# Loading expert weights of a mixture-of-experts kernel in 16 KB rows, one expert's matrix per transfer, and giving ring places back whole

## The reference

```python
def hierarchical_moe(h, w_group, b_group, w_router, b_router, w_gate, w_up, w_down):
    ...
    e_id = g_idx[:, None] * EXPERTS_PER_GROUP + top_i.astype(jnp.int32)
    ...
    def expert_block(args):
        xb, e = args
        return (jax.nn.silu(xb @ w_gate[e]) * (xb @ w_up[e])) @ w_down[e]
    ys = lax.map(expert_block, (xs, block_e)).reshape(P, D)
    out = jnp.zeros((N, D), ys.dtype).at[slot_tok].add(ys * slot_w[:, None].astype(ys.dtype))
```

## Time and profile before

| | |
|---|---|
| median of 3 runs | 1418.24 us (1414.12 to 1418.97) |
| span of the profiled execution, first to last instruction | 1412.1 us |
| expert loop of layer 0, of layer 1 | 207.4 to 689.0 us, 915.7 to 1397.0 us |
| TensorE busy | 1298.4 us, 92% |
| weight load busy | 638.1 us, 45% |
| VectorE, ScalarE, GpSimd busy | 34%, 16%, 3% |
| moved by DMA | 489.84 MB, mean 347 GB/s |
| expert weights | 3 x 64 transfers of 2048 KB for each matrix kind, 402.7 MB in 192 transfers |

### The profile page before, as it was taken

The page is one execution under the profiler, slowest core; times in us unless marked ns, Lnnn a source line. Parts: engine busy times, 40 slices in busy tenths (PEclk is TensorE's granted clock), DMA queues, the critical chain, the costliest instruction groups (busy, mean ns, idle before and its releaser), DMA issues.

```text
span 1412.1 us, 17373 instructions
## 1 busy us (share of the span) xinstructions
PE 1298.4 (92%) x6934; PEld 638.1 (45%) x6934; DVE 480.3 (34%) x1239; ACT 227.7 (16%) x523; POOL 35.6 (3%) x75
## 2 busy tenths in 40 slices
PE   5998979999899999899889999889998999998998
PEld 3875543334344334334368555433334333334433
DVE  1188253333323333333311143542323232323232
ACT  1013341000100000100223244310001000001000
POOL 1001120000000000000000000200000000000000
PEclk8999999999999999999999999899999999999999
DMA  9968358999999999999973373579999999999980
GB/s 343 382 229 334 158 233 334 417 415 421 418 413 418 415 420 420 418 413 374 408 278 119 119 312 165 235 294 413 417 419 420 418 414 417 420 418 416 417 353 31
DMA packets 82589, 489.84 MB, mean 347 GB/s; under 512 B 11489, under 2 KB 11634, under 8 KB 33394
## 3 DMA queue, kind: packets, MB, share of 16 engines
q1 hardware_dynamic: 76480, 486.62, 84.4%
q10 hardware_dynamic: 6066, 2.64, 0.7%
HBM read 488.20 MB, written 1.05 MB: 346 GB/s over the span
## 4 chain that ended last, share of the span: by engine, by line
PE 77%; ACT 7%; DVE 7%; issue 3%; ACTq 2%; SPq 1%; DMA 1%; POOL 0%; DVEq 0%
PE psum L1256 77%; ACT phase_region L703 3%; DVE phase_region L905 3%; ACTq L539 2%; DVE x_tokens L1069 2%; ACT phase_region L712 1%; DMA weight_ring<-in_w_ada 1%; SPq L422 1%; ACT phase_region L715 1%; PE psum L1318 0%; ACT ada_partials L582 0%; ACT h_or_mix_T L574 0%; ACT phase_region L563 0%; DVE phase_region L840 0%; ACT phase_region L717 0%
## 5 line engine op out<-in xcount | busy, mean ns | idle before, releaser
L1256 PE MATMUL psum<-weight_ring,phase_region 128*64 128x512 f32 (+1 forms) x3264 | 700.8, 600 | 64.6 <-ACT phase_region L715 41.6
L1256 PEld LDWEIGHTS psum<-weight_ring,phase_region 128*64 128x64 f32 (+1 forms) x3264 | 243.3, 136 | 490.7 <-issue 440.5
L1256 PE MATMUL psum<-phase_region 128*128 128x128 bf16 (+4 forms) x2064 | 255.3, 284 | 5.2 <-POOL phase_region L492 0.9
L1256 PEld LDWEIGHTS psum<-phase_region 128*128 128x128 bf16 (+2 forms) x2064 | 153.2, 117 | 135.3 <-issue 85.3
L1122 DVE TENSOR_TENSOR phase_region<-psum,gate_rows 128x512 f32<-128x512 f32 x64 | 44.3, 692 | 238.6 <-PE psum L1256 238.6
L1256 PE MATMUL psum<-h_or_mix_T,weight_ring 128*128 128x256 f32 (+1 forms) x520 | 117.3, 385 | 5.5 <-DVE h_or_mix_T L849 3.4
L703 ACT ACTIVATE phase_region<-psum,shift,scale 128x128 f32<-128x128 f32 x136 | 51.2, 457 | 439.0 <-PE psum L1256 439.0
L1256 PEld LDWEIGHTS psum<-h_or_mix_T,weight_ring 128*128 128x128 f32 x520 | 100.6, 198 | 19.6 <-DVE h_or_mix_T L849 3.5
L1115 DVE SCALAR_TENSOR_TENSOR phase_region<-phase_region,psum 128x512 f32<-128x512 f32 x32 | 33.7, 1054 | 205.2 <-PE psum L1256 205.2
L1256 PE MATMUL psum<-weight_ring,h_or_mix_T 128*128 128x512 f32 x224 | 102.7, 610 | 0.0
L1069 DVE TENSOR_TENSOR x_tokens<-psum,x_tokens 128x512 f32<-128x512 f32 x136 | 93.6, 690 | 24.6 <-PE psum L1256 24.6
(11 more groups left out here) (172 smaller groups left out, 559.6 us busy)
## 6 DMA issues: line engine op xcount, KB each, us to landing
weight_ring<-in_moe_w_gate SPq DMA_DIRECT2D x64, 2048.0 KB, 9.4
weight_ring<-in_moe_w_up SPq DMA_DIRECT2D x64, 2048.0 KB, 12.5
weight_ring<-in_moe_w_down SPq DMA_DIRECT2D x64, 2048.0 KB, 11.5
weight_ring<-in_w_ada SPq DMA_DIRECT2D x12, 3072.0 KB, 13.0
weight_ring<-in_w_ada SPq DMA_DIRECT2D x12, 1024.0 KB, 15.8
weight_ring<-in_odd_w_in SPq DMA_DIRECT2D x6, 2048.0 KB, 12.6
weight_ring<-in_even_w_in SPq DMA_DIRECT2D x4, 2048.0 KB, 23.6
weight_ring<-in_even_w_out SPq DMA_DIRECT2D x2, 2048.0 KB, 9.9
```

Of the source, the lines that this page charges most:

```text
L1256: return pe.matmul(out_, lhsT, rhs, start=first, stop=last, **kw)
```

## The change

A transfer now brings the whole matrix of one expert, 16 KB a partition in one row; the slab of a pair is still two transfers of 2 MB on the same two semaphores. SyncE issues both when the whole slab has been used; the semaphores `half_used` are gone. TensorE waits for both transfers before the first product of a slab, and `narrow` runs all k for output half 0, then all k for output half 1.

```diff
-                words = slice(half * KD * F // 2, (half + 1) * KD * F // 2)
-                sp.dma_start(pair_slab(n)[:, :, words], src[L, :, bass.ds(pair * 2, 2), words]).then_inc(
+                sp.dma_start(pair_slab(n)[:, half:half + 1, :], src[L, :, bass.ds(pair * 2 + half, 1), :]).then_inc(
                     (slab_in, rest_in)[half][n % RING], 16)
...
                     pairs = turn * UNROLL + (EP * L + k // 3 + 1)
-                    sp.wait_ge(half_used[k % 3], pairs)
-                    load_pair_half(L, k + RING, 0, turn * UNROLL + (k + RING) // 3)
                     if k % 3 < 2:
                         sp.wait_ge((gate_done, up_done)[k % 3], pairs)
                     else:
                         sp.wait_ge(down_done, pairs * 2)
-                    load_pair_half(L, k + RING, 1, turn * UNROLL + (k + RING) // 3)
+                    for half in range(2):
+                        load_pair_half(L, k + RING, half, turn * UNROLL + (k + RING) // 3)
...
-                def widen(bank, w, xt, done, half=None, second=None):
+                def widen(bank, w, xt, done):
 
                     for k in range(KD):
-                        if second is not None and k == KD // 2:
-                            pe.wait_ge(*second)
                         for e in range(2):
                             ins = mm(PS[e * SLOT:(e + 1) * SLOT, bank, :], xt[:, k, e * SLOT:(e + 1) * SLOT],
                                      w[:, e, k * F:(k + 1) * F], k == 0, k == KD - 1, skip_group_check=True)
-                        if half is not None and k == KD // 2 - 1:
-                            ins.then_inc(half, 1)
                     ins.then_inc(done, 1)
...
                         pe.wait_ge(slab_in[slabs[0] % RING], land[0])
-                        widen(0, pair_slab(slabs[0]), XT[:, j % 2], gate_done, half_used[0],
-                              (rest_in[slabs[0] % RING], land[0]))
+                        pe.wait_ge(rest_in[slabs[0] % RING], land[0])
+                        widen(0, pair_slab(slabs[0]), XT[:, j % 2], gate_done)
...
                         pe.wait_ge(slab_in[slabs[2] % RING], land[2])
-                        for h in range(2):
-                            ins = narrow(pair_slab(slabs[2]), range(KF // 2), h, None)
-                        ins.then_inc(half_used[2], 1)
                         pe.wait_ge(rest_in[slabs[2] % RING], land[2])
                         for h in range(2):
-                            narrow(pair_slab(slabs[2]), range(KF // 2, KF), h, down_done)
+                            narrow(pair_slab(slabs[2]), range(KF), h, down_done)
```

More of the change, by code:

```diff
@@ L263, in build_trunk @@
         xt_act = sem("xt_act")
-        half_used = [sem(f"{w}_half_used") for w in ("gate", "up", "down")]
         gate_done = sem("gate_done")
@@ L1599, in moe @@
                         pe.wait_ge(slab_in[slabs[1] % RING], land[1])
-                        widen(1, pair_slab(slabs[1]), XT[:, j % 2], up_done, half_used[1],
-                              (rest_in[slabs[1] % RING], land[1]))
+                        pe.wait_ge(rest_in[slabs[1] % RING], land[1])
+                        widen(1, pair_slab(slabs[1]), XT[:, j % 2], up_done)
                         pe.wait_ge(slots_built, i * (2 * UNROLL) + 2 * ((EP + 1) * L + j + 2))
```

## The result

The changed kernel takes 1431.31 us in the median (1430.27 to 1432.62), the kernel before 1418.28 us; the ratio is 1.0104, with an interval of 1.0082 to 1.0126. It is slower by 13 us, where I had forecast no change, 1418 us in a range of 1410 to 1427.

A forecast was written before the change was run, and what follows sets the result against it. TensorE's own chain, 30.14 us a pair, was taken as the bound, with DMA only keeping up. The 1412.1 us span plus 0 for each of five points, with the median 6.1 us above, gave 1418 us, range 1410 to 1427.

The forecast's parts named there:

- point 2: TensorE waiting for both transfers before a slab: cost 0; bounds a gain of 0, a loss of 11 us.
- Point 1: SyncE's later issue of a slab's first transfer: 0 on the path, at least 13.8 us in hand at every slab.
- Point 3: SyncE's longer wait: only the same slab's two transfers queue behind it, cost 0.
- Point 4: Order of `narrow`: VectorE's first evacuation can start 3.7 us after down starts instead of 5.4; gain 0.
- Point 5: 16 KB rows: 426 GB/s, 7.7 ns fixed cost a packet, 11.8 us of DMA time saved, 0 on the path.
- The sign by which I meant to see it: DMA share in a mid-loop pair down from 1.00 to about 0.98 while GB/s stays.
- A: Rival: 16 KB rows run slower, below 405 GB/s TensorE waits in the loops; 1440 or 1467 us; chance 0.11.
- B: Rival: DMA truly bounds the loops, so its 11.8 us saving comes back, 1406 us; chance 0.06.
- C: Rival: ring reserve smaller than worked out, DMA pauses over 14 us stop TensorE; 1425 us or more; chance 0.02.
- D: Rival: scatter alone carries the median over 7 us in either direction; chance 0.01 each way.
- weight-load rule: Skill's rule judging TensorE by its weight loads' busy share, here 45%, so not full; the prediction didn't follow it.

The follow-up runs named there:

- experiment 6: Changed kernel with only the wait for the down slab's second transfer moved ahead of the slot-weight waits: 1418.31 us, ratio 1.0012.
- experiment 2: Changed kernel with 8 KB rows of both experts per transfer again, all else as changed: 1430.59 us, ratio 1.009.
- experiments 9 and 10: ScalarE copies the turned operands before spreading tokens: on the changed kernel 1386.57 us, ratio 0.9794; on the kernel before 1385.18 us, ratio 0.9792.
- Experiments 4 and 7: Changed kernel with SyncE's first load held back: 1432.26 us; kernel before with one idle extra wait at the head of down: 1429.91 us.
- 3: Kernel before with TensorE waiting for the down slab's second transfer at its head: 1427.30 us, ratio 1.0068.
- experiment 1: Changed kernel with both waits for the down slab moved ahead of the slot-weight waits: 1421.77 us, ratio 1.0022.
- experiment 8: Kernel before with its one wait for the down slab's first transfer moved ahead of the slot-weight waits: 1417.63 us, ratio 1.0007.
- experiment 11: Kernel before with three more waits, on semaphores reached at program start, at the head of every down slab: 1415.79 us, ratio 0.9999.

## Why the prediction was wrong

**The step that failed is point 2.** "Does a fulfilled wait itself cost?" I answered it from a row in which the three waits of down and gate lie inside a run of products, and there they cost nothing (13.95 us). The new wait lies at the head of down, behind a wait that TensorE really waits for, and there it adds 0.10 us to the gap (1.97 against 1.87 us). The quoted order showed this: the register instruction with the operands' waits, and the product with two waits behind it. I read it for what was waited for, and not for what has to be done after the release. I had the two gaps in front of me too: the earlier trace rows has 1.7 and 1.9 us, a difference between pairs that I did not ask about. Its cost as such is small, 8 x 0.1 us. The rest comes by the clock: 5 falls x 1.70 us = 8.5 us, together 9.3 us, against 9.2 us by which the loops grew in the windows (4.0 + 5.2). My bound for this point, 0.12 us for a slab and 11 us in all, comes near the loss only by luck: it stood for a cost of the waits themselves in 96 slabs, and the runs show 0.8 us for that.

**The clock was read as a constant.** I noted 1.00 in the earlier trace rows as a fact of the loop; it was a state that held by about 0.1 us of gap (none of 1.87 us brought a fall, 34 of 48 of 1.97 us did). No rival had the clock in it.

**Point 1 held.** Two issues take 0.87 us, as the queue of the changed kernel shows; landing took at most 16.0 us, where I had 16.4:

```profile
417.66 0.87 SPq L386 DMA_DIRECT2D weight_ring<-in_moe_w_down  x2
...
DMA to landing us min/median/max: 7.5/11.7/16.0
```

**Point 3 held**: experiment 6 keeps it and costs nothing. **Point 4 held**: the first evacuation starts 3.69 us after down, the combine when down ends:

```profile
1414.29 7.09 PE L1253 MATMUL psum<-weight_ring,phase_region 128*64 128x512 f32 x32 [1.73 <-ACT phase_region L712]
...
1421.31 3.96 PE L1253 MATMUL psum<-phase_region 128*128 128x512 f32 x8
...
1417.98 0.69 DVE L1119 TENSOR_TENSOR phase_region<-psum,gate_rows 128x512 f32<-128x512 f32 x1 [4.67 <-PE psum L1253]
```

**Point 5 held**: 429 GB/s measured, 426 forecast, and zero on the path. The fixed cost of a packet worked out from the saturated rates is 2 x 8192 x 16 / 422 - 16384 x 16 / 429 = 10.1 ns. It hangs on one GB/s: other stretches of the same loops show 427 and 428 GB/s in 16 KB rows, against 422 in 8 KB rows, which gives 7 to 9 ns. So my 7.7 ns can stand. The Trainium skill ("DMA: Bandwidth & Descriptors", Why small descriptors are slow) has about 3 cycles a packet, 3.5 ns by the estimate of the prediction; the measurement is larger and decides. The sign by which I meant to see it failed: the DMA share of a mid-loop pair stayed at 1.00.

**Rivals.** A, slower rows, fell with 429 GB/s and experiment 2. B, DMA as the true bound, fell with experiments 9 and 10: a shorter gap alone made both faster by 2.1%. C, a smaller reserve, fell: no slab was waited for. D, scatter, fell: all runs of the changed kernel, in two series, lie between 1428.89 and 1432.62 us. My answer to the weight-load rule in B, to go by the timeline's holes, was right as to the bound. The slower result had none of the reasons I had priced.

**What stays open.** In the first two traces the loops explain 9.2 of 13.0 us. The head, 4.2 us longer there, is chance: in the repeated traces the first gate slab starts at 215.62 us in the kernel before and at 212.60 us in the changed one. Between these repeats the loops, with six falls, account for 11.2 of the 11.7 us of span (first gate slab to last down slab, 5.6 us more in each layer). Between the loops the changed kernel took 4.8 us more (231.5 against 226.7 us), with 41 us of low clock against 27. The repeats have 41 and 31 us. Experiments 4 and 7 have 41 as well, but 2 and 3, with falls in the loops too, have 31. Without falls in the loops it is 27 to 31 us, and 38 in experiment 1. It may be that falls in a loop change how the following part meets the clock; these traces don't settle it. Nor is it shown why a gap of 1.97 us has a fall behind it in one pair and none in the next such pair.

## What to carry to other kernels

Where an engine really waits, what stands between the release and its first product is on the path: look in the trace which instructions run there, and put waits that are surely fulfilled, and register work, ahead of the one that holds. Read the gap again afterwards: experiment 8 did this and gained nothing. A short gap in TensorE that recurs in a loop can be a tenth of a microsecond away from a fall of its clock, so compare the gap's length pair by pair and the granted clock by stretches, not by their means. And an even gap that a trace shows in every round can be worth more than the detail of the transfers: here the reordering of ScalarE's steps gave 2.1%, the longer rows nothing.

## What the runs showed of the hardware

A gap of 1.97 us in TensorE's products, after the 48 products of gather and six transposes, was followed by 3.4 us at 1.2 GHz in 34 of 48 cases, and gaps up to 1.87 us there in none. The Trainium skill ("TensorE: Matmul & The Clock Gate", Why this matters for your kernels) warns of long idle gaps between bursts of matmuls, since they cost the full clock. The trace agrees in kind, but 1.97 us is shorter than the gaps that section warns of.

One core reached 427 to 429 GB/s in 16 KB rows and 422 GB/s in 8 KB rows (experiments 9 and 10). The Trainium skill ("HBM Reference", Specifications (TRN2)) has about 425 GB/s for a core that streams alone; the trace agrees.

A fulfilled wait cost nothing inside a run of products (13.95 us for down and gate with three of them) and nothing ahead of a wait that holds (experiment 11), but 0.10 us as an instruction of its own between the release and the first product (gap of 1.97 us instead of 1.87).
